# Moving two plain projections into the seven-product scheme, and a group's first products ahead of its start

## The reference

```python
shift, scale, gate = split(silu(c) @ w_ada + b_ada, 3)
h = rmsnorm(x, g_pre) * (1 + scale) + shift
hc, bc, cc, gc, q, k, v, ga = split(h @ w_in)        # eight parts, 512 columns each
u = cc * hc
conv_y = sum(conv_w[i] * u_pad[:, i:i + L] for i in range(3))
ya = rmsnorm(bc * conv_y, g_conv) * silu(gc)
o = stick_breaking(q, k, v, b_sb)                    # causal, 8 heads of 64
yb = rmsnorm(o, g_attn) * silu(ga)
y = x + gate * rmsnorm(concat([ya, yb]) @ w_out, g_post)
return y, k, v, last rows of u                       # for prompt and decode
```

## Time and profile before

| | us |
|---|---|
| median of 3 executions | 829.97 (826.9 to 831.13) |
| the profiled execution | 829.45 |
| its span, first to last instruction | 827.7 |
| TensorE busy | 786.0 |
| VectorE busy | 537.8 |
| GpSimd busy | 429.5 |
| ScalarE busy | 352.2 |

### The profile page before, as it was taken

The page is one execution under the profiler, slowest core; times in us unless marked ns, Lnnn a source line. Parts: engine busy times, 40 slices in busy tenths (PEclk is TensorE's granted clock), DMA queues, the critical chain, the costliest instruction groups (busy, mean ns, idle before and its releaser), DMA issues.

```text
span 827.7 us, 14401 instructions
## 1 busy us (share of the span) xinstructions
PE 786.0 (95%) x4397; PEld 522.3 (63%) x4397; DVE 537.8 (65%) x728; ACT 352.2 (43%) x729; POOL 429.5 (52%) x230
## 2 busy tenths in 40 slices
PE   0889989999999999999999999999999999999995
PEld 0455766766787666768866766788676665444442
DVE  3575679787585888848748877585788854232344
ACT  7311065775122667821155676112567731122122
POOL 0105896474787566666966485588665630100000
PEclk9989999999999999999999999999999999999998
DMA  8998777577789888786998776868978797554001
GB/s 317 359 340 293 224 229 223 177 239 230 239 256 305 268 257 266 242 253 211 299 282 262 244 259 222 274 212 289 302 250 255 232 332 304 166 182 163 27 27 53
DMA packets 131071, 197.85 MB, mean 239 GB/s; under 512 B 10025, under 2 KB 51030, under 8 KB 130994
## 3 DMA queue, kind: packets, MB, share of 16 engines
q1 hardware_dynamic: 99512, 181.11, 66.5%
q10 hardware_dynamic: 31482, 15.82, 6.8%
HBM read 185.25 MB, written 11.66 MB: 238 GB/s over the span
## 4 chain that ended last, share of the span: by engine, by line
PE 79%; issue 5%; DMA 5%; DVE 4%; POOL 3%; SPq 2%; ACT 0%; ACTq 0%; POOLq 0%; DVEq 0%
PE ps L1359 76%; DMA ring<-in_w_ada_dram 4%; PE ps L1599 3%; POOL prod L617 2%; SPq L386 1%; DVE ps L1243 1%; DMA ring<-in_cache_k_dram 1%; SPq L378 1%; DVE zd L1219 1%; DVE zc L1249 0%; POOL wsl L600 0%; DVE rows L1062 0%; DMA ring<-in_cache_v_dram 0%; DVE zc L1229 0%; POOL spd L560 0%
## 5 line engine op out<-in xcount | busy, mean ns | idle before, releaser
L617 POOL TENSOR_TENSOR prod<-ring,qb 128x1024 f32<-128x1024 f32 x128 | 308.7, 2430 | 195.2 <-DMA ring<-in_cache_k_dram 92.0
L1359 PE MATMUL ps<-hT,wsl 128*128 128x258 f32 (+1 forms) x640 | 174.7, 419 | 0.1
L1219 DVE TENSOR_REDUCE zd<-prod 128x16 f32<-128x1024 f32 x128 | 154.3, 1213 | 26.0 <-POOL prod L617 25.4
L1359 PEld LDWEIGHTS ps<-hT,wsl 128*128 128x128 f32 x640 | 119.1, 190 | 53.3 <-issue 18.6
L1359 PE MATMUL ps<-ring,apad 128*32 128x512 f32 x592 | 84.4, 650 | 9.0 <-DMA ring<-in_w_ada_dram 7.5
L1359 PE MATMUL ps<-xT,wS 128*128 128x258 f32 x352 | 92.2, 385 | 0.0
L1359 PE MATMUL ps<-xT,wsl 128*128 128x258 f32 x352 | 89.5, 386 | 0.0
L1229 DVE TENSOR_SCALAR zc<-ps,bsb 128x512 f32<-128x512 f32 (+3 forms) x96 | 54.8, 612 | 42.0 <-PE ps L1359 41.7
L657 ACT ACTIVATE rise<-ps,bsh 128x512 f32<-128x512 f32 (+3 forms) x96 | 55.5, 578 | 45.9 <-DVE zc L1229 45.8
L1359 PEld LDWEIGHTS ps<-xT,wsl 128*128 128x128 f32 x352 | 62.9, 190 | 18.7 <-issue 8.0
L657 ACT ACTIVATE av<-ps 128x512 f32<-128x512 f32 (+3 forms) x96 | 46.8, 488 | 63.4 <-PE ps L1599 62.9
(11 more groups left out here) (241 smaller groups left out, 1012.7 us busy)
## 6 DMA issues: line engine op xcount, KB each, us to landing
ring<-in_cache_k_dram SPq DMA_DIRECT2D x256, 256.0 KB, 3.5
ring<-in_cache_v_dram SPq DMA_DIRECT2D x256, 256.0 KB, 3.2
wsl<-in_w_in_dram ACTq DMA_DIRECT2D x30, 512.0 KB, 6.5
ring<-in_w_ada_dram SPq DMA_DIRECT2D x5, 2048.0 KB, 14.7
xT<-in_x_prompt_dram SPq DMA_DIRECT2D x2, 2048.0 KB, 10.9
out_dram<-oT SPq DMA_DIRECT2D x8, 512.0 KB, 5.0
ring<-in_x_prompt_dram SPq DMA_DIRECT2D x8, 512.0 KB, 7.2
xT<-y_parts SPq DMA_DIRECT2D x6, 512.0 KB, 9.5
```

The lines of the kernel that those rows point to most:

```text
L617: pool.tensor_tensor(prod[:, p % 2].rearrange("p (j c) -> p j c", j=2), kring[:, p % 4], qb[:, p // 16].unsqueeze(1).to_broadcast([P, 2, H ...
L1219: v.tensor_reduce(zd[:, t // 16, :, r:r + 2], prod[:, t % 2].rearrange("p (j h d) -> p h j d", j=2, h=NH), AX_X, ALU.add)\
L1359: return nc.tensor.matmul(out, l, r, start=start, stop=stop, skip_group_check=True)
```

## The change

V and B become a pair of their own, the second of now four: (Q, K), (V, B), (GC, GA), (HC, CC). A group has 8 chunks (`CHUNKS`) instead of 6. V then comes with the channels as rows of the tile, in `vT`, which shares `av`'s space, and is turned by eight transposes in `value_rows(0)` at slot 7 and `value_rows(1)` at slot 9; ScalarE copies them to `vN` (`value_rows_copy`). The decode rows of V are turned beside K's in key_rows(2). Products 1, 5, 2, 6 of the next group's chunk 0 (`AHEAD`) stand in slots 32 and 33, where B was, and so do their weight sums on GpSimd. The slots ahead of the attention hold the rest. In the last group, where there is no next group, the first two k-steps of `out_unit(2)` stand there, the transfers for it are issued in another order, and a part of the gated outputs comes back to the ring of the key pages instead of `yT`. `gp` (the post-norm gain times gate) moves from `wS` to `gab` in the first group, since `wS` is now wanted earlier.

The diff, cut to its core:

```diff
-SLABS = ((0, 1), (0, 3), (1, 2))
+SLABS = ((0, 1), (2, 3), (0, 1), (2, 3))
+PAIRS = 4
+CHUNKS = 2 * PAIRS
-EARLY = ((), (1, 5), (2, 6), (3, 7, 11), (4, 15), (12, 16), (13, 17))
+AHEAD = (1, 5, 2, 6)
+EARLY = ((3, 7, 11), (4, 15, 12, 16), (13, 17, 21), (14, 25, 22, 26), (23, 27, 31), (24, 35), (32, 36), (33, 37))
+EARLY_FIRST = {6: (21, 25, 22, 26, 23, 27, 31), 7: (24, 35, 32, 36, 33, 37)}
+TAKEN = {1: (4, 11, 15, 12, 16), 3: (14, 21, 25, 22, 26), 5: (24, 31, 35), 6: (32, 36)}
+TAKEN_FIRST = {6: (21, 25, 22, 26), 7: (24, 31, 35, 32, 36)}
+SUMMED = {1: 0, 3: 1, 5: 2, 8: 3}
+SUMMED_FIRST = {7: 2, 8: 3}
...
+        gp = gab[:, 0:D]
+        gp_end = wS[:, 1:3, :].rearrange("p a c -> p (a c)")
+        vT = av[:, :, :].rearrange("p a c -> p (a c)")
+        def cumulate_bank(g, k):
+            return BX if k == 0 else Z if g < GROUPS - 1 else BY
...
# SyncE, last group and after it
+                    if last and t == 26:
+                        sp_e.wait_ge(st_full[2], CHUNKS * GROUPS - 4)
+                        load_wo(WO_ORDER[0])
+                        sp_e.wait_ge(st_full[4], CHUNKS * GROUPS - 4)
+                        load_wo(WO_ORDER[1])
...
+            sp_e.wait_ge(prod_ready, 32 * GROUPS - 3)
+            load_part(1, 0)
+            sp_e.wait_ge(st_full[5], ALL)
+            load_part(0, 0)
+            load_part(0, 1)
+            sp_e.wait_ge(prod_ready, 32 * GROUPS - 2)
+            load_part(1, 1)
             sp_e.wait_ge(z_full, NU * GROUPS)
             load_wo(WO_ORDER[2])
             load_wo(WO_ORDER[3])
...
# GpSimd
-                    if not first and t in (0, 1):
-                        weight_sum(g, 0, 2 + t)
+                    if t == (5 if first else 2):
+                        weight_sum(g, 1, 0)
+                        weight_sum(g, 1, 1)
+                    if t == (6 if first else 3):
+                        weight_sum(g, 1, 2)
+                        weight_sum(g, 1, 3)
                     for p in pairs_at(t):
...
+                if not last:
+                    weight_sum(g + 1, 0, 0)
+                    weight_sum(g + 1, 0, 1)
                 silu_mul(g, 1)
                 decode_scores(g, 1, first)
                 if not last:
-                    weight_sum(g + 1, 0, 0)
+                    weight_sum(g + 1, 0, 2)
                 decode_softplus(g, 1)
                 if not last:
-                    weight_sum(g + 1, 0, 1)
+                    weight_sum(g + 1, 0, 3)
...
# ScalarE
+                    for code in (TAKEN_FIRST if first else TAKEN).get(t, ()):
+                        evac_st(g, code // 10, code % 10)
                     if t == 7:
-                        evac_v(g, first, 1)
+                        value_rows_copy(g, first, 0)
                         key_rows_copy(g, 0, first)
+                    if t == 9:
+                        value_rows_copy(g, first, 1)
...
# VectorE
+                    chunk = (SUMMED_FIRST if first else SUMMED).get(t)
                     if u > 0 and u % 6 == 0:
+                        chunk = 3 + u // 6
+                    if chunk is not None:
+                        product_sum(g, first, chunk, 3)
+                        product_sum(g, first, chunk, 7)
...
# TensorE
+                def value_rows(c):
+                    if c == 0:
+                        pe.wait_ge(e_c11, CHUNKS * g + 2)
+                        if not first:
+                            pe.wait_ge(a_ready, NU * g)
+                    else:
+                        pe.wait_ge(d_c12, CHUNKS * g + 2)
+                        pe.wait_ge(pj_free, PJ * g + 1)
+                    for j in range(4):
+                        t = 4 * c + j
+                        last = nc.tensor.transpose(ps[:, Z + 2, P * j:P * (j + 1)], vT[:, P * t:P * (t + 1)], ident[:, :])
+                    last.then_inc(pj_full, 1)
...
                 for t in range(8):
-                    if t == 7:
-                        values(1)
-                    elif t == (6 if first else 0):
-                        values(0)
...
+                    for code in EARLY_FIRST.get(t, ()) if first else EARLY[t]:
+                        product(g, code // 10, code % 10)
                     if t == 7:
+                        value_rows(0)
                         key_rows(0)
+                        product(g, 4, 1)
                     if first and t in (1, 5):
                         gate_strips(t // 5)
                     if first and t in (2, 6):
                         gate_sums(t // 6)
...
+                    if t == 9:
+                        value_rows(1)
                     if u < NU:
                         for i, j, ks in pieces_at(u)[0]:
+                            product(g, i, j, ks)
+                    elif last_:
+                        if u == NU:
+                            out_unit(2, (0, 1), True)
                     else:
-                        project_b(u - NU, range(0, 4))
+                        product(g + 1, 0, AHEAD[2 * (u - NU)])
...
+                    if u == 2:
+                        pe.wait_ge(pj_free, PJ * g + 2)    # in scores(u)
```

More of the change, by code:

```diff
@@ L64 @@
 PART = [4, 5, 6, 3, 7, 0, 2, 1]
-PJ = 6
+PJ = 2
 MS = 5
@@ L114, in pieces_at @@
     step, chunk = ("open", "mid")[i] if i < 2 else i % 3, 2 + i // 3
-    return [[(chunk + back, j, ks) for back, j, ks in piece] for piece in PIECES[step][2 * (u % 2):2 * (u % 2) + 2]]
+    return [[(chunk + 2 + back, j, ks) for back, j, ks in piece] for piece in PIECES[step][2 * (u % 2):2 * (u % 2) + 2]]
 def quad_of(slot):
@@ L767, in evac_st @@
                 if j == 1:
-                    if not (first and i == 2):
+                    if n:
                         act.wait_ge(e_c21, n)
@@ L912, in body @@
                         for back, j in {0: ((-1, 4), (0, 1)), 1: ((0, 5), (0, 2), (0, 6)), 2: ()}[i % 3]:
[L913 to L914 removed]
+                            evac_st(g, 4 + i // 3 + back, j)
                     if first and t in (1, 5):
```

407 lines of the change are left out of this document (178 added, 229 removed).

## The result

| | us |
|---|---|
| median after, 4 executions | 849.0 (843.86 to 852.86) |
| before, beside it | 829.64 (826.9 to 831.13) |
| ratio, 95% interval | 1.023 (1.0203 to 1.0256): slower |
| the profiled execution after | 843.86, its span 841.7 |
| forecast | 840, range 822 to 849 |

The side was right; the time stands on the upper end of the range, and the medians lie 19.4 us apart where the sum had 10.4. The profiled execution is the fastest of the four, 14.4 us over that of before; both differences have to be explained.

A forecast was written before the change was run, and what follows sets the result against it. TensorE, busy 95% of the span, was taken as the bound. Terms -21.7 + 15.7 + 2.3 - 1.0 + 6.6 + 7.7 + 0.8 = +10.4 on 829.45 gave 840 us, range 822 to 849.

The forecast's parts named there:

- TensorE's work: Each group: 30.9 us removed, 25.5 added, so -5.4 a group, -21.7 for four; TensorE's busy time 17 to 22 lower.
- First group: Slots before attention: slot 8 starts at 130.8 instead of 106.9, with 8.5 us of work and 15.7 of three waits.
- Wait one: First group: TensorE waits 6.2 us ahead of product 25 for GpSimd's first sum, queued behind pairs 0 to 9.
- Wait two: First group: TensorE waits 1.9 us ahead of product 23 for GpSimd's third sum, behind pairs 10 and 11.
- Wait three: First group: TensorE waits 7.6 us ahead of product 24 for VectorE's product_sum(2), behind gates(1) and two reductions.
- Clock: Half clock behind the first group's waits: 0.6 and 1.7 us, together 2.3, from nothing to 3.4; 0.8 at the end.
- Start of attention: Groups 1 to 3: SyncE waits for V's copy, delaying key loads; 1.9 us a group, with 0.3 for earlier slots +6.6 altogether.
- pairs bound each group: Rival, groups 1 to 3: five sums among fourteen GpSimd pairs push reductions past slot 8; +8 us, 848; chance 0.1.
- The row of comparison: GpSimd's 4.55 us wait before pair 15, read as slack for four added sums of 5.1; 0.3 a group taken.
- Last group: Early out_unit(2) steps wait 6.2 us for transfers, decode_softplus shifts 1.5: +7.7, from 3 to 11, plus 0.8 for the clock.
- The first group doesn't hold TensorE: Rival: the first group's three waits and their clock, 18.0 us, fall away, giving 822; chance 0.17.
- Half of the waits: Rival: last group's loads land at 4.6 us and group starts absorb SyncE's delay, -5 to -10: 830 to 834; chance 0.2.

The follow-up runs named there:

- experiment 1: Changed kernel with gate_sums(1) ahead of the products of slot 6 on TensorE in the first group, instead of behind them; 836.64 us, ratio 1.0107.
- Experiments 1 to 4: Reorderings of the changed kernel's first group; the one without its own line moves only GpSimd's (V, B) sums to slots 3 and 4: 839.54 us, ratio 1.0113.
- experiment 3: Changed kernel with gate_sums(1) ahead of slot 6's products and the (V, B) sums two slots earlier on GpSimd, first group; 837.56 us, ratio 1.0116.
- Experiment 5: Changed kernel with 14 and 12 unread filler matmuls ahead of products 25 and 24 of the first group, to price the clock; 845.38 us, ratio 1.0187.
- experiment 6: Changed kernel with V's output issued at SyncE's slot 12 instead of 10, behind the key loads of pairs 16 and 17; 843.34 us, ratio 1.0171.
- experiment 9: The changed kernel run once more, unaltered; 850.38 us, ratio 1.0228, profiled execution 851.87.
- experiment 10: Changed kernel with the four weight sums of V and B in groups 1 to 3 cut to 16 columns, results wrong; 840.2 us, ratio 1.0129.
- experiments 11 and 12: Both build on experiment 8; the first loads pair 16's key pages ahead of four value loads on SyncE: 820.07 us, ratio 0.9893; the second is under experiment 12.
- Experiment 7: Changed kernel with the first two k-steps of out_unit(2) in the last group moved behind outputs(22), just ahead of cumulate(1); 843.55 us, ratio 1.0149.
- experiment 8: Changed kernel with the edits of experiment 4, experiment 6 and Experiment 7 together; 819.45 us, ratio 0.9869.
- experiment 4: As experiment 3, with VectorE's product_sum(2) at slot 5 instead of 7 in the first group, ahead of gates(1); 831.69 us, ratio 1.003.
- experiment 12: As experiment 8, with GpSimd's four weight sums of V and B at slots 3 and 4 in every group; 819.5 us, ratio 0.986.

## Why the side was right, and where the sum fell short

**TensorE's work.** The size of the stretches fits 5.4 a group: group 2 came out at -3.5 with 1.4 more of waits in it (2.5 against 1.1), so 4.9 of work. The busy time is no measure of it (9.6 less, not 17 to 22 as I announced), since records at the half clock are longer: by 1.8 and 1.7 behind the two waits of the first group, 2.7 at the end and 2.6 in group 1, which is 8.8 and brings the difference to 18.4.

**First group, +18.25 against 18.6.** Wait one was 7.42 and not 6.2: product 21 ended 0.5 earlier and the sum 0.5 later. Wait two, 1.9, did not appear. Product 25 ran at half clock and TensorE came to 23 at the moment the third sum ended (GpSimd's row L635 is 102.62 and 1.26 long); I had charged the clock behind wait one with 0.6 on top. Together it is 7.42, 1.82 of slow clock (3.56 - 1.74) and 0.19 ahead of 23, 9.4 against 8.7. Wait three was 6.00 and not 7.6: gates(1) took 3.96 to the next reduction, since GpSimd stood idle; I had taken 5.0 to 5.5, down from a row in which both worked (in experiment 1, beside a working GpSimd, it took 5.88). The clock behind it cost 3.46 - 1.74 = 1.7, as forecast. All of this comes to 17.15 against 18.0, by misses of opposite sign. And the 130.8 for slot 8 doesn't come out of the forecast's own terms, which give 106.9 + 8.5 + 15.7 = 131.1, 133.4 with the clock; measured is 132.29. Experiments 1 to 4 show the rest of this step: the mechanism, product_sum(2) behind gates(1) behind gate_sums(1), was right, and experiment 3 adds what I had not seen, that the key products on GpSimd can hold the same place.

**Clock.** Twice 0.50 of full speed behind the two waits and 1.7 each, as the rows of before had it. The rule that the Trainium skill states in "TensorE: Matmul & The Clock Gate", section "Part 1: The HAM clock gate", and that the prediction set beside this term, agrees with that. Experiment 5 is the test: 1.8 to 3.1 us in the traces and 3.6 by the ratios, against the 2.3 that I gave it. What I left at nothing is the clock behind the waits at the start of attention, 2.6 in group 1 of after.

**Start of attention: the step that failed.** I took 1.9 a group, "SyncE's queue issues V's output at 424.39, and must now wait for the copy: 1.8 later". SyncE does wait for that copy in the first group (experiment 6), where I hadn't counted it, and in none of groups 1 to 3, where I had. I had left SyncE where it was, 50.6 behind `cumulate(1)`, and moved the copy only. In group 1 of after the copy ends at 53.2 and SyncE comes to the output at 54.6, 3.6 later than before. So something else had made SyncE late. The chain that the traces show, in us behind `cumulate(1)` of group 0, before and after:

| | before | after |
|---|---|---|
| pair 4 starts on GpSimd | 9.9 | 15.5 |
| SyncE is through with y_parts of slot 6 | 31.7 | 37.4 |
| SyncE issues the loads of pair 16 | 52.7 | 56.2 |
| they land after | 3.5 and 3.9 | 4.7 and 6.5 |
| pair 16 starts on GpSimd | 57.1 | 63.4 |

In groups 2 and 3 pair 16 starts at 58.1 and 57.7 before, and at 62.1 and 62.4 after. Pair 4 comes 5.6 later: pair 2 already starts 1.5 later (5.8 against 4.3), and two of the new sums with the second's wait for TensorE take 4.1. The ring of four buffers hands this on to SyncE, which waits 3.7 for GpSimd; and between slots 6 and 11 SyncE hasn't the time to make it good. In after it waits for nothing there. The longest gap between two of its loads, 2.56 inside the row at 273.41 above, is register loads, one of 1.81 where most take 0.48. Before it had a gap of 3.3, 260.88 to 264.21 (SyncE's queue of the kernel before, group 1), and 1.8 of it was a wait for TensorE to free a buffer of value pages:

```profile
259.99 0.89 SPq L386 DMA_DIRECT2D ring<-in_cache_k_dram  x2
264.21 3.31 SPq L386 DMA_DIRECT2D ring<-in_cache_v_dram  x4
267.57 0.43 SPq L446 DMA_DIRECT2D out_dram<-vN  x1
269.21 3.13 SPq L386 DMA_DIRECT2D ring<-in_cache_k_dram  x4
```

The reduction of pair 16 stands in VectorE's queue ahead of the log weights. How much was it? I had 6.6 for three groups. The stretches of groups 1 to 3 sum to -1.2 where I had -4.7, so the profile of after says 10.1, and that of experiment 9, whose three groups are 3.8 longer, 13.9. Of the 10.1, 6.6 are the longer waits for the log weights (9.6 against 3.0), and 2.6 the half clock behind the one of 3.62. That the waits alone grew by just what I had is luck, since it came by another way.

The length of the four sums is 3.2 of the one and 6.9 of the other (the three groups of experiment 10 against both), 8.2 by the ratios. That is the rival "pairs bound each group" (0.1, 848, price 8), working within the forecast's other terms, but it isn't the whole: with the sums cut short pair 4 starts only 1.0 earlier (14.5), since the wait for product 16 stays, and pair 16 at 62.6, 61.1 and 62.2. With V's output moved and the sums as they were (experiment 6) it starts at 61.8, 60.8 and 61.0, so the place of the output has a part in it as well. What experiment 10 leaves, 4.8 more of waits than before (7.8 against 3.0), experiments 11 and 12 only place: neither another order on SyncE nor an earlier start on GpSimd alone takes it away, so what both share, the stretch of SyncE's queue from pair 12 to pair 18, is the likeliest holder. That is argued from their rows; no run made this queue shorter. That the landing is longer because of a slab that is now loaded shortly ahead of it (issued at 287.22, 3.8 ahead; before at 261.88, 7.3 ahead) is read from the traces and wasn't tried. So in groups 1 to 3 the cause of these waits is shown in part, and the rest stays open.

**The row of comparison.** I had read the wait of 4.55 us ahead of pair 15's product in group 2 as slack for the added sums. It is slack of GpSimd only. The queue behind it, SyncE's, had 1.8 in group 1 (the wait within the gap of 3.3), and 2.6 and 1.3 in groups 2 and 3.

**Last group.** 4.39 and 1.09 were measured where I had 6.2 and 1.5. The clock cost 2.7 and not 0.8: the first six records took 5.3 (692.70 to 697.99) where six at full clock take 2.6 (0.86 for two), so the sum is 8.2 against 8.5. TensorE waited once, at the start, and the slow clock covered the second wait. Experiment 7 shows that half a slot is enough to hide most of it.

**Why the median is 5 above the profiled execution.** Experiment 9 shows where such an execution is longer, in the prologue and at the starts of attention, and that it comes back in another set of four. Why the same program waits 1.8 us in one execution and 4.0 in the next isn't settled. A part of it is the clock: in experiment 9 it fell behind two of these waits (3.33 and 4.00), in after behind one (3.62). SyncE without slack is in keeping with it, but shows nothing: experiment 8 still has that queue and spreads over 5 us, experiment 4 over 12, and before over 6.6 beside them.

**The rivals.** "The first group doesn't hold TensorE" fell with the first row of it. "Half of the waits" was wrong for the first group and for the end: the transfers for out_unit(2) landed 5.7 to 10.0 after their issue and not 4.6 (issued from 684.92 on, the last needed one landed at 697.68), and the wait was smaller only because the slow clock covered the second part.

## What to carry to other kernels

- When work is moved to where it depends on more, write down for each queue what stands ahead of the instruction that releases it. Here one wait could come about in two queues: the move that removed it alone no longer did so beside a second move; five small moves of order, costing no work, turned 2.3% slower into 1.3% faster.
- Slack has to be looked for in the last queue of the chain. GpSimd waiting 4.55 us said nothing of SyncE, whose time went in register loads and page loads back to back; instructions added on the one were paid in part on TensorE, through the other.
- When a new wait is priced, price the clock behind it as well. At the start of attention it fell to half behind the wait of 3.62 and stayed at full speed behind that of 2.10 in experiment 6, and this was worth more (2.6) than the wait that was saved (1.5).
- A wait that is covered by another, or by a slow clock, comes out when that one is removed: 1.9 after the sums were moved, 1.79 after the fillers. Undo pairs of suspects together before adding up their single gains.

## What the runs showed that I had not expected

- A short wait can cost most of its length again. In experiment 12 an idle time of 2.16 us in group 3 was followed by this (stretch, busy, granted clock, DMA share, GB/s):

```profile
594.00:596.00 2.00, 2.00 (x7) 0.55 0.98 326
596.00:598.00 2.00, 2.00 (x8) 0.60 0.85 271
```

  while idle times of 2.98 and 3.08 us at the same place in experiments 7 and 4 were followed by turns at full length (0.55 for three). The length of the wait alone doesn't say whether the clock falls.
- The slower clock can hide a dependence (product 23), so that its cost isn't simply added to that of the wait.
- SyncE needed about 1.2 us between two groups of page loads for the registers with the page numbers (289.74 to 290.97 in experiment 6), and now and then up to 2.9, when the register load took 1.8 to 2.2 in place of 0.48. A pair of key pages with 0.9 of issue costs the queue 2.1.
